# A last layer norm in two layouts: the last token group normalised with tokens on partitions, and earlier row stores

## What is computed

```python
def layer_norm(x, g, b):
    mu = jnp.mean(x32, -1, keepdims=True)
    xc = x32 - mu
    var = jnp.mean(xc * xc, -1, keepdims=True)
    return xc * lax.rsqrt(var + LN_EPS) * g + b

def swiglu(x, wg, wu, wd):
    return (jax.nn.silu(x @ wg) * (x @ wu)) @ wd

def ffn_sublayer(x, wg, wu, wd, g, b):
    return layer_norm(DN_ALPHA * x + 0.5 * swiglu(x, wg, wu, wd), g, b)

hp = ffn_sublayer(yp, ffn1_wg, ffn1_wu, ffn1_wd, ln1_g, ln1_b)   # hs likewise
mp, ... = mixer_prompt(hp, ...)                                  # ms, ... = mixer_sample(hs, ...)
hp = layer_norm(DN_ALPHA * hp + mp, ln2_g, ln2_b)
yp = ffn_sublayer(hp, ffn2_wg, ffn2_wu, ffn2_wd, ln3_g, ln3_b)   # -> y_prompt; ys -> y_sample
```

## Time and profile before

| | |
|---|---|
| time, three runs | 2738.99 us median (2737.57 to 2739.33) |
| profiled execution | 2739.62 us, its span 2737.8 us |
| PE busy | 2592.4 us, 95% of the span |
| DVE busy | 1532.2 us, 56% |
| ACT busy | 667.7 us, 24% |
| POOL busy | 543.0 us, 20% |

### The profile page before, as it was taken

How to read it: one execution, slowest core, us unless ns; L and a number is a source line. 1 busy time by engine, 2 the same in 40 slices (tenths; PEclk the granted TensorE clock), 3 DMA queues, 4 the chain that set the end, 5 groups by cost and what they waited for, 6 DMA issues and landing times.

```text
span 2737.8 us, 42508 instructions
## 1 busy us (share of the span) xinstructions
PE 2592.4 (95%) x16993; PEld 2363.6 (86%) x16993; DVE 1532.2 (56%) x3027; ACT 667.7 (24%) x1520; POOL 543.0 (20%) x526
## 2 busy tenths in 40 slices
PE   8989999999999979998898789999999999999996
PEld 8989999999998737897676667768999999999995
DVE  5544465446542187797778866326563555355533
ACT  1110122012201265661221156402220121012102
POOL 5220233023301011110000022313330233023300
PEclk9999999999999999999999899999999999999998
DMA  7455246524652112320010022004464346434631
GB/s 186 123 142 140 74 125 174 137 74 124 176 135 63 47 43 86 108 78 1 2 32 1 2 63 60 21 8 117 124 177 116 89 128 176 117 89 128 176 101 48
DMA packets 456067, 260.63 MB, mean 95 GB/s; under 512 B 21672, under 2 KB 448792, under 8 KB 455872
## 3 DMA queue, kind: packets, MB, share of 16 engines
q1 hardware_dynamic: 448432, 237.43, 33.1%
q0 software_dynamic: 7440, 20.49, 2.7%
HBM read 251.07 MB, written 6.81 MB: 94 GB/s over the span
## 4 chain that ended last, share of the span: by engine, by line
PE 80%; DVE 13%; issue 4%; ACT 2%; DMA 1%; SPq 1%; DVEq 0%; ACTq 0%
PE ps L1656 33%; PE ps L1722 20%; PE ps L518 8%; PE ps L523 5%; PE ps L848 4%; PE ps L583 2%; PE ps L642 1%; PE ps L739 1%; DVE down_weights L1108 1%; PE ps L713 1%; PE ps L574 1%; DVE aux L1280 1%; PE ps L726 1%; DMA weight_ring<-ffn_wu 1%; DVE weight_ring L1365 1%
## 5 line engine op out<-in xcount | busy, mean ns | idle before, releaser
L1656 PE MATMUL ps<-aux,big 128*128 128x172 f32 x2112 | 333.5, 311 | 14.7 <-ACT big L1854 14.6
L2031 DVE TENSOR_TENSOR weight_ring<-ps,big 128x172 f32<-128x172 f32 x396 | 123.8, 331 | 386.5 <-ACT big L1854 350.7
L1656 PE MATMUL ps<-acts,weight_ring 128*128 128x172 f32 x2112 | 323.3, 311 | 11.4 <-DMA weight_ring<-ffn_wg 6.6
L1656 PEld LDWEIGHTS ps<-aux,big 128*128 128x128 f32 x2112 | 315.8, 191 | 19.9 <-ACT big L1854 17.9
L1656 PE MATMUL ps<-weight_ring 128*128 128x172 f32 x2112 | 329.5, 309 | 0.0
L1656 PEld LDWEIGHTS ps<-acts,weight_ring 128*128 128x128 f32 x2112 | 314.4, 192 | 13.1 <-DMA weight_ring<-ffn_wg 6.9
L1656 PEld LDWEIGHTS ps<-weight_ring 128*128 128x128 f32 x2112 | 313.8, 190 | 0.0
L1722 PE MATMUL ps<-big 128*128 128x172 f32 x1584 | 238.8, 309 | 0.0
L1722 PEld LDWEIGHTS ps<-big 128*128 128x128 f32 x1584 | 233.1, 190 | 0.0
L518 PE MATMUL ps<-acts,weight_ring 128*128 128x344 f32 x768 | 231.3, 457 | 0.0
L2183 POOL TENSOR_TENSOR big<-weight_ring 128x512 f32<-128x512 f32 x66 | 83.6, 1267 | 667.7 <-PE ps L1656 620.7
(11 more groups left out here) (331 smaller groups left out, 3696.8 us busy)
## 6 DMA issues: line engine op xcount, KB each, us to landing
weight_ring<-ffn_wg SPq DMA_DIRECT2D x132, 512.0 KB, 5.3
weight_ring<-ffn_wu SPq DMA_DIRECT2D x132, 512.0 KB, 7.0
down_weights<-ffn_wd SPq DMA_DIRECT2D x24, 1408.0 KB, 11.7
weight_ring<-ffn_wd SPq DMA_DIRECT2D x24, 1408.0 KB, 9.8
weight_ring<-w_in SPq DMA_DIRECT2D x9, 1024.0 KB, 5.3
weight_ring<-w_in SPq DMA_DIRECT2D x8, 512.0 KB, 5.4
weight_ring<-w_out SPq DMA_DIRECT2D x4, 1024.0 KB, 6.1
out_y_prompt<-weight_ring SPq DMA_DIRECT2D x8, 512.0 KB, 2.6
```

What stands on the lines that cost most here:

```text
L1656: last = M(PS[:, 3 * m + bank, 0:QW], lhs[:, i, :], rhs[:, i, :], start=begin and i == 0, stop=end and i == KH - 1, skip_group_check=True)
L2031: V.tensor_tensor((CG, CU)[m][:, (out, i)[m], :], PS[:, 3 * m + bank, 0:QW], ST[:, m, part, :], ALU.add)\
```

## The change

The last norm group is no longer normalised feature-major. The tokens up to 688 (groups 0 and 1) are normalised as before and turned out as blocks 0 to 5, the last of which has 48 rows. Two blocks are turned after each of the down pairs 0, 1 and 2, and none after down pair 3. The raw columns of tokens 688 to 1031 are then turned first, in three blocks of 128, 128 and 88 rows, into banks 0 to 5, and normalised with tokens on partitions: the mean and the sum of squares come from ACT's accumulator output along the free dimension, DVE centres and applies the gain, and then the reciprocal root and the bias. Gain and bias rows are loaded once, broadcast over the partitions, into slot 1 of the weight ring. POOL's sums and PE's two mean products for group 8 are gone. SP stores blocks 0 and 1 between its last two down loads.

```diff
+        RAW0 = 2 * TW
+        RAW_ROWS = (P, P, TOK - RAW0 - 2 * P)
+        RAW_OUT = (AUX[:, 0:D], AUX[:, D:2 * D], XOUT[:, 0, :])
+        ROW_JUNK = TMP[:, 1536:1536 + D]
+        LNG, LNB = RING[:, 1, 0:D], RING[:, 1, D:2 * D]
+        def row_stats(r):
+            return (SMALL[0:RAW_ROWS[r], 4 * r + i:4 * r + i + 1] for i in range(4))
+        def raw_rows(r):
+            return PS[0:RAW_ROWS[r], 2 * r:2 * r + 2, :].rearrange("p u c -> p (u c)")
...
 @@ SP @@
+            def store_block(b):
+                sp.wait_ge(y_copied, 2 * b + 2)
+                rows = min(P, RAW0 - b * P)
+                sp.dma_start(O["y_prompt"][0, b * P:b * P + rows, :], XOUT[0:rows, b % 2, :]).then_inc(y_stored[b % 2], 16)
...
+                    if ff and g == 2:
+                        sp.wait_ge(up_mm, up_count(6 * FP - 1, 4, 1))
+                        for dst, name in ((LNG, "ln3_g"), (LNB, "ln3_b")):
+                            sp.dma_start(dst, I[name][0].rearrange("(o d) -> o d", o=1).to_broadcast([P, D])).then_inc(ring_in[1], 16)
                     down_load(ff, g, 2)
+                    if ff and g == 2:
+                        for b in range(2):
+                            store_block(b)
                     down_load(ff, g, 3)
...
-            for b in range(9):
-                sp.wait_ge(y_copied, 2 * b + 2)
-                if b < BLK:
-                    sp.dma_start(O["y_prompt"][0, b * P:b * P + P, :], XOUT[:, b % 2, :]).then_inc(y_stored[b % 2], 16)
-                else:
-                    sp.dma_start(O["y_sample"][:, 0, :], XOUT[0:NB, b % 2, :]).then_inc(y_stored[b % 2], 16)
+            for b in range(2, 6):
+                store_block(b)
+            for r in range(2):
+                sp.wait_ge(ln_done, 8 + r + 1)
+                sp.dma_start(O["y_prompt"][0, RAW0 + P * r:RAW0 + P * r + P, :], RAW_OUT[r]).then_inc(y_stored[1], 16)
+            sp.wait_ge(ln_done, 11)
+            last = SEQ - RAW0 - 2 * P
+            sp.dma_start(O["y_prompt"][0, RAW0 + 2 * P:SEQ, :], RAW_OUT[2][0:last]).then_inc(y_stored[0], 16)
+            sp.dma_start(O["y_sample"][:, 0, :], RAW_OUT[2][last:last + NB]).then_inc(y_stored[0], 16)
...
 @@ PE @@
-                pe.wait_ge(ln_done, 8 if b < 5 else 9)
+                pe.wait_ge(ln_done, 8)
...
+            def turn_raw(r):
+                pe.wait_ge(z_done, z_before(2, 3))
+                at = RAW0 + P * r
+                for d in range(DT):
+                    last = T(PS[0:RAW_ROWS[r], 2 * r + d // 4, P * (d % 4):P * (d % 4) + P], ACTS[:, d, at:at + RAW_ROWS[r]], IDENT[:, :])
+                last.then_inc(y_turned, 1)
...
                     for jd in range(4):
                         down_pair(ff, g, jd)
-                        if ff and g == 2:
-                            turn_out(jd)
-                            if jd == 3:
-                                turn_out(4)
+                        if ff and g == 2 and jd < 3:
+                            turn_out(2 * jd)
+                            turn_out(2 * jd + 1)
...
-            pe.wait_ge(y_copied, 10)
-            mean(8)
-            var(8)
-            for b in range(5, 9):
-                turn_out(b)
+            for r in range(3):
+                turn_raw(r)
...
 @@ ACT @@
...
-                            store_rows(jd)
-                            if jd == 3:
-                                store_rows(4)
+                            store_rows(2 * jd)
+                            store_rows(2 * jd + 1)
...
-            square(8)
-            sd(8)
-            gain(8)
-            for b in range(5, 9):
-                store_rows(b)
+            for r in range(3):
+                rows, ps = RAW_ROWS[r], raw_rows(r)
+                neg_mean, ssq, root, _ = row_stats(r)
+                act.wait_ge(y_turned, 12 + r + 1)
+                A(ROW_JUNK[0:rows], ps, ACT.Copy, scale=-1.0 / D, accum_out=neg_mean).then_inc(ln_mean, 1)
+                act.wait_ge(ln_mean, 8 + r + 1)
+                A(ROW_JUNK[0:rows], ps, ACT.Square, bias=neg_mean, accum_out=ssq).then_inc(ln_sq, 1)
+                act.wait_ge(ln_sq, 8 + r + 1)
+                A(root, ssq, ACT.Sqrt, scale=1.0 / D, bias=EPS[0:rows, 0:1]).then_inc(ln_sd, 1)
...
 @@ DVE @@
-            centre(8)
-            sqsum(8)
-            scale(8)
+            dve.wait_ge(ring_in[1], up_reach(1, 2, LAST, 1) + 32)
+            for r in range(3):
+                rows, ps, out = RAW_ROWS[r], raw_rows(r), RAW_OUT[r]
+                neg_mean, _, root, rstd = row_stats(r)
+                dve.wait_ge(ln_sq, 8 + r + 1)
+                if r == 2:
+                    dve.wait_ge(y_stored[0], 16 * 3)
+                link(V.scalar_tensor_tensor(out[0:rows], ps, neg_mean, LNG[0:rows], ALU.add, ALU.mult))
+                dve.wait_ge(ln_sd, 8 + r + 1)
+                link(V.reciprocal(rstd, root))
+                V.scalar_tensor_tensor(out[0:rows], out[0:rows], rstd, LNB[0:rows], ALU.mult, ALU.add).then_inc(ln_done, 1)
...
 @@ POOL @@
-                    sums(2 * ff, g)
+                    if not (ff and g == 2):
+                        sums(2 * ff, g)
```

More of the change, by code:

```diff
@@ L1599, in _ @@
                     up_load(1, 0, 1)
-            for b in range(9):
-                sp.wait_ge(y_copied, 2 * b + 2)
-                if b < BLK:
-                    sp.dma_start(O["y_prompt"][0, b * P:b * P + P, :], XOUT[:, b % 2, :]).then_inc(y_stored[b % 2], 16)
-                else:
-                    sp.dma_start(O["y_sample"][:, 0, :], XOUT[0:NB, b % 2, :]).then_inc(y_stored[b % 2], 16)
+            for b in range(2, 6):
[7 more added lines that the diff above has]
+            sp.dma_start(O["y_sample"][:, 0, :], RAW_OUT[2][last:last + NB]).then_inc(y_stored[0], 16)
             sp.wait_ge(y_stored[0], 16 * 5)
-            sp.wait_ge(y_stored[1], 16 * 4)
+            sp.wait_ge(y_stored[1], 16 * 5)
         @block.tensor
@@ L1763, in turn_out @@
             def turn_out(b):
-                rows = P if b < BLK else NB
-                pe.wait_ge(ln_done, 8 if b < 5 else 9)
+                rows = min(P, RAW0 - b * P)
+                pe.wait_ge(ln_done, 8)
                 for half in range(2):
```

## The result

The changed kernel took 2721.44 us (median of 4 runs, 2718.71 to 2723.82) beside 2738.28 us for the kernel before (4 runs). The ratio is 0.9944, 95% interval 0.9931 to 0.9956: 0.56% faster. The forecast was 2725.0, so the direction was right and the time came out 3.6 us lower.

A forecast was written before the change was run, and what follows sets the result against it. It took the serial tail after PE's last product as the place to gain: 18.3 us less there, 4.1 given back in the gaps, so 14.2 off, 2725.0 us forecast, range 2721.5 to 2730.5.

The forecast's parts named there:

- What bounds, and the sum: Tail after PE's last product: shrinks from 35.25 to 16.9 us; gaps give back 4.1, so the span falls 14.2 us.
- The gaps: Between down pairs: a second turned block costs 1.38 us in each of three gaps, 4.14 us in all.
- SP's queue: Gain and bias loads and the stores of blocks 0 and 1, put among the down loads, cost nothing.
- The tail's terms: After PE's last product: residual, raw turns, ACT's and DVE's work per block, last store; 16.9 us to the end.
- the drain that the Trainium skill adds: Behind ACT's table load for the root: 1380 ns by the skill's page, making the sum 1.4 us longer; not charged.
- Dear handoffs: Tail: each of six uses of an accumulator column as bias pointer costs half a us more, 2728 us; 10%.
- The clock: PE's clock drops in the gaps (5.2 us) and on the first raw block (0.9 us), 2731 us; 7%.
- rival 3: PE's clock falls in a gap and stays at 1.2 GHz through a down pair: 22.5 us, 2747 us; 3%.
- Rival 4: No measurable change: gaps cost 12.8 us, for instance if ACT's copy of block 4 waited for block 2's store; 3%.

The follow-up runs named there:

- free banks: Changed kernel with the second block of each gap turned into the two banks the down pair in front has just left: 2720.33 us, ratio 0.9934.
- new norm alone: Changed kernel with one block a gap, blocks 3 to 5 turned after down pair 3, all stores behind the last load: 2719.60 us, ratio 0.9944.
- late stores: Changed kernel with the stores of blocks 0 and 1 issued behind the last down load instead of between the last two: 2736.78 us, ratio 1.0003.
- other two comparisons: The changed kernel, unchanged, measured twice more beside the kernel before: 2722.54 us (ratio 0.9949) and 2722.30 us (ratio 0.9951).
- early turning alone: Kernel before with blocks 0 and 1, 2 and 3, and 4 turned after down pairs 0, 1, 2, two stores between loads: 2739.22 us, ratio 1.0011.

## Why the prediction was right, and where it was off

**What bounds, and the sum.** The serial tail was the place. Predicted was a tail of 16.9 us and a price of 4.14 us in the gaps; measured 16.96 and 4.26. The change in the last stretch is 14.03 us, where the forecast said 14.2. So the mechanism and its size were right for what the change touches.

**The gaps.** The price of 1.38 for a second block, read from blocks 3 and 4, held within 0.1: it was 1.47, 1.41 and 1.38. The free banks show that the wait for the copy made 0.5 to 0.6 us of each gap.

**SP's queue.** Cost nothing, as predicted: load and stores are across by 2646, where I said 2648, and DVE reads the weights at 2649.97. I mentioned that ACT's copy of block 2 waits for the store of block 0, but gave no price to it: the place of the stores is what keeps the second block of a gap from costing 16 us. With one block a gap the late place is hidden: the new norm alone has its stores behind the last load, and PE goes from pair to pair there with 0.87 us between.

**The tail's terms.** PE's last product to ACT's first copy: 1.92 us, predicted 1.89. From there to the end of DVE's last operation: 11.73, predicted 12.08; a block on ACT took 2.57 instead of 2.67, the pointer square 1.11 where I took 1.148. From there to the end of the span: 3.3, predicted 2.9. The two errors cancel, which is luck. Nearly a tenth of a us of the first is the sum's own: by the earlier trace rows the copy with its read comes to 1.105 us and the square with its read to 1.23, not 1.12 and 1.25, for each of two blocks. That DVE and not ACT would set the last block, by 0.2 us, is seen at 2716.01: ACT's last sum of squares was there at 2715.82. The table load took 1.28 and the root followed 1.29 after its start, as in the earlier trace rows; the drain that the Trainium skill adds (ScalarE: Activation LUTs, What ACT_TABLE_LOAD costs) doesn't show here either.

**The rivals.** Dear handoffs: refuted, ACT's square starts 0.02 us after the accumulator read. The clock: refuted in the windows of the changed kernel. The first row is the third gap, the others the tail:

```profile
2681.00:2682.00 1.00, 0.66 (x7) 0.39 (x5) 0.97 (x3) 0.98 (x2) 0.00 (x0) 1.00 0.00 0
...
2705.00:2706.00 1.00, 0.20 (x2) 0.08 (x2) 0.67 (x2) 0.00 (x0) 0.00 (x0) 1.00 0.00 0
...
2710.00:2712.00 2.00, 0.00 (x0) 0.00 (x0) 1.65 (x3) 1.99 (x4) 0.00 (x0) 1.00 0.00 0
```

The granted clock stays at 1.00 through the raw turns and beyond, and between the pairs. With it falls rival 3. Rival 4 named a mechanism that exists, a copy that waits for a store behind the weights, but at a place where it is covered: the store of block 2 issues at 2659.08, the bus is down to 8 GB/s from 2670 on, and ACT copies block 4 at 2680.89. The late stores show the price where it isn't covered.

**What was off.** The median of the first comparison fell by 16.8 us. In its profile 1.67 of that lie ahead of the last down group, and 1.1 are not in the profile. In the other two comparisons it fell by 13.6 and 13.4. No term of the sum was mis-sized by more than 0.4 us. What was wrong is in the bounds: the sum was hung on one profiled execution in which the last down group started at 2610.09, the latest of twelve, and on the median beside it, and the range had no term for the spread of some 6 us in that start. The first measurement fell to the very edge of the range by some 3 us that two repeats didn't show, so they are put down to this spread and not to the change.

## What to carry to other kernels

Where the last norm has no work behind it, its length is a chain of single operations. Here the layout in which statistics fall out of the free dimension halved the tail (35.25 to 16.96 us), even with the turning put first. Work that is pushed from the tail into a dense stretch is paid in full there: the 4.3 us spent in the gaps bought 3.4 back. What helped was to give it banks of its own, and to lay one block beside ACT's and DVE's work on the raw blocks, where PE stood idle; two blocks there gained 0.3 us in all. When a buffer is reused sooner, look up where its store stands in the queue; the place of two stores decided over as much as the whole change.

## What the runs showed beyond that

A long pause of PE can cost twice. After the 13.3 us of standing in the kernel with late stores the next pair took 24.44 us instead of 22.46, with the clock first at 0.50, and the 2.88 us of waiting in front of the mean product made it 1.48 us instead of 0.84. I had expected neither at this size. The short pauses of the changed kernel, 0.40 us in a gap and 0.80 us in front of the raw turns, left the clock at 1.00. So did the 16 turned tiles that stand in front of the mean product in the kernel before: from the last product of down pair 3 to that mean product it is 3.0 us there, and 2.9 us in the kernel with the early turning alone. The clock was 1.00 with the tiles in between and 0.50 without them.
